# A fused layer with a routed mixture of experts: filler products once, the second expert's gathers behind the first's, and the fourth expert's table and gathers ahead of the first additions

## The reference, cut to what matters

```python
gate = jnp.sum(jax.nn.one_hot(top_idx, N_EXPERTS, dtype=jnp.float32) * top_w[..., None], axis=1)
y = jnp.zeros_like(t)
for e in range(N_EXPERTS):
    h = jax.nn.silu(t @ w1[e]) * (t @ w3[e])
    y = y + gate[:, e:e + 1] * (h @ w2[e])
x = layer_norm(ALPHA * x + y, ln2_g[l], ln2_b[l])
```

## Time and profile before

| | |
|---|---|
| median of 3 runs | 1004.55 us (1002.58 to 1005.56) |
| profiled execution | 1000.43 us |
| its span, first to last instruction | 998.8 us |
| mean granted TensorE clock | 0.975 of full speed |
| TensorE busy | 933.8 us, 93% of the span |
| VectorE, ScalarE, GpSimd busy | 606.9, 476.0, 200.1 us |

### The profile page before, as it was taken

How to read it: one execution, slowest core, us unless ns; L and a number is a source line. 1 busy time by engine, 2 the same in 40 slices (tenths; PEclk the granted TensorE clock), 3 DMA queues, 4 the chain that set the end, 5 groups by cost and what they waited for, 6 DMA issues and landing times.

```text
span 998.8 us, 19152 instructions
## 1 busy us (share of the span) xinstructions
PE 933.8 (93%) x7424; PEld 755.2 (76%) x7424; DVE 606.9 (61%) x793; ACT 476.0 (48%) x758; POOL 200.1 (20%) x244
## 2 busy tenths in 40 slices
PE   8999999999999999889998999899999999999930
PEld 7778998986777777668886678688888888888820
DVE  3203724655655664766656857577777777777728
ACT  3312622235655555551212446466666666666614
POOL 3000000000000000020000476634433333332116
PEclk9999999999999999989999999999999999999975
DMA  9301210002000301159332479999999999999656
GB/s 259 62 22 43 59 48 22 1 2 63 22 22 24 78 17 43 43 191 365 128 127 85 114 223 296 298 319 314 314 312 325 317 317 323 302 321 324 185 157 251
DMA packets 102666, 168.18 MB, mean 168 GB/s; under 512 B 25777, under 2 KB 49329, under 8 KB 102609
## 3 DMA queue, kind: packets, MB, share of 16 engines
q1 hardware_dynamic: 88768, 145.05, 43.0%
q0 software_dynamic: 10800, 21.17, 9.0%
q10 hardware_dynamic: 3040, 1.19, 0.6%
HBM read 142.84 MB, written 24.54 MB: 168 GB/s over the span
## 4 chain that ended last, share of the span: by engine, by line
PE 82%; DVE 5%; DMA 4%; POOL 4%; ACT 3%; issue 2%; SPq 0%; POOLq 0%; ACTq 0%; DVEq 0%
PE bank L705 14%; PE bank L707 13%; PE bank L706 13%; PE pz L705 6%; PE pz L707 6%; PE pz L706 6%; PE pz L1041 5%; PE pz L1083 3%; PE pz L821 3%; PE bank L901 3%; PE bank L917 2%; DMA tab<-slot_tokens 1%; POOL slot_tokens L581 1%; PE bank L1030 1%; DVE cstat L1784 1%
## 5 line engine op out<-in xcount | busy, mean ns | idle before, releaser
L1635 DVE TENSOR_TENSOR el<-er,eh 128x1024 fp32r<-128x1024 f32 x192 | 225.3, 1222 | 53.6 <-ACT eh L1334 53.1
L1334 ACT ACTIVATE eh<-er 128x1024 fp32r<-128x1024 f32 x192 | 190.4, 1052 | 0.0
L1568 DVE TENSOR_TENSOR_SCAN Qs<-Qs 128x128 f32<-128x128 f32 (+7 forms) x48 | 65.0, 1354 | 74.0 <-ACT Qs L1221 74.0
L705 PE MATMUL bank<-xT_hi,w_hi 128*128 128x512 f32 (+1 forms) x264 | 105.5, 400 | 1.9 <-DVE xT_lo L1453 1.9
L707 PE MATMUL bank<-xT_hi,w_lo 128*128 128x512 f32 (+1 forms) x264 | 101.7, 385 | 0.0
L705 PE MATMUL pz<-eh,xh 128*128 128x512 f32 x256 | 101.6, 397 | 0.0
L706 PE MATMUL bank<-xT_lo,w_hi 128*128 128x512 f32 (+1 forms) x264 | 101.3, 384 | 0.0
L706 PE MATMUL pz<-el,xh 128*128 128x512 f32 x256 | 99.8, 390 | 0.0
L707 PE MATMUL pz<-eh,xl 128*128 128x512 f32 x256 | 99.7, 389 | 0.0
L550 POOL MEMSET rw<- 128x128 f32 x1 | 0.2, 205 | 419.8 <-ACT aT L1262 419.8
L705 PE MATMUL bank<-w_hi,xT_hi 128*128 128x384 f32 x192 | 65.0, 338 | 1.3 <-ACT kteN L1236 1.3
(11 more groups left out here) (274 smaller groups left out, 1825.6 us busy)
## 6 DMA issues: line engine op xcount, KB each, us to landing
er<-in_w_dram SPq DMA_DIRECT2D x192, 512.0 KB, 9.6
w_raw<-in_w_in_dram SPq DMA_DIRECT2D x21, 512.0 KB, 4.0
x_row<-in_x_dram SPq DMA_DIRECT2D x8, 512.0 KB, 8.9
xres<-in_x_dram SPq DMA_DIRECT2D x8, 512.0 KB, 5.2
x_scratch<-x SPq DMA_DIRECT2D x8, 512.0 KB, 2.8
sum_scratch<-x SPq DMA_DIRECT2D x8, 512.0 KB, 3.9
cx<-sum_scratch SPq DMA_DIRECT2D x8, 512.0 KB, 6.5
out_dram<-cx SPq DMA_DIRECT2D x8, 512.0 KB, 2.6
```

The source lines that it names most:

```text
L705: pe.matmul(dst, lh, rh, start=(k == k_first), stop=False)
L1334: act.activation(eh[:, p, :], er[:, p, :], ACT.Copy).then_inc(S["eh_ok"], 1)
L1568: dve.tensor_tensor_scan(Qs[:, h, 0:W][:, ::-1], Qs[:, h, 0:W][:, ::-1], Qs[:, h, 0:W][:, ::-1], 1.0, ALU.mult, ALU.min).then_inc(S["scan_ ...
L1635: dve.tensor_tensor(el[:, p, :], er[:, p, :], eh[:, p, :].bitcast(F32), ALU.subtract).then_inc(S["el_ok"], 1)
```

## The change

1. `spin(34)` is taken out of `slot_tokens` and stands once, after the first two calls. The third call, in block 0, has none behind it.
2. `xgA` and `xgB` have a second pair of buffers, used by block 1. GpSimd issues block 1's gathers as soon as block 0's have landed, ahead of both scatters.
3. `slotG` has a second buffer, used by block 1.
4. Once the lists are written, GpSimd's order becomes: tables of 3, 0 and 1; quarters of 3, 0 and 1 (each waits for all three tables); gathers of 3; gates of 0 and 1; additions of 0; table and quarters of 2; additions of 1. Then `step` as before.
5. `gather` waits also for all earlier gathers to have landed.

```diff
-            for b in range(DIRECT):
...
+            def first_gather(b):
+
+                pool.wait_ge(S["first_ok"], 2 * b + 2)
+                for buf, src, ids in ((xgAs[b % 2], x1_dram, firstA), (xgBs[b % 2], x1_quarters, firstB)):
                     pool.indirect_dma_start(buf[:, :], None, src, bass.IndirectOffsetOnAxis(ids[:, b:b + 1], 0)).then_inc(S["xg_in"], 16)
+
+            first_gather(0)
+            pool.wait_ge(S["xg_in"], 32)
+            first_gather(1)
+            scatter(0)
+            scatter(1)
+            pool.wait_ge(S["xtr_ps"], NXR)
+            pool.wait_ge(S["xg_in"], 64)
+            first_gather(2)
...
             def pool_pass(j):
                 b0 = NE * j
-                load_table(0, b0)
-                load_table(1, b0 + 1)
-                quarters(0, b0, 2)
-                quarters(1, b0 + 1)
...
+                if isinstance(j, int):
+                    for r in (3, 0, 1):
+                        load_table(r, b0 + r)
+                    for r in (3, 0, 1):
+                        quarters(r, b0 + r, b0 + 3)
+                    gather(3, b0 + 3, 0, b0 + 1)
+                    gates(0, b0)
+                    gates(1, b0 + 1, 1)
+                    add_rows(0, b0)
+                    load_table(2, b0 + 2)
+                    quarters(2, b0 + 2, b0 + 4)
+                    add_rows(1, b0 + 1, 1)
...
                 last.then_inc(S["sids_ps"], 1)
-                if b:
-                    spin(34)
 
             for b in range(2):
                 slot_tokens(b)
+            spin(34)
```

More of the change, by code:

```diff
@@ L254, in build @@
         tabQ = [small(f"tabQ{r}", [P, 1], U32) for r in range(4)]
-        slotG = small("slotG", [P, 2])
+        slotGs = [small(f"slotG{r}", [P, 2]) for r in range(2)]
         quad = small("quad", [P, 1])
@@ L296, in build @@
         el = at("el", 48 * K, [P, NPIECE, D], F32R)
-        xgA = rt("xgA", 6 * K, [P, D])
-        xgB = rt("xgB", 10 * K, [P, DQ])
+        xgAs = [rt("xgA0", 6 * K, [P, D]), rt("xgA1", 42 * K, [P, D])]
+        xgBs = [rt("xgB0", 10 * K, [P, DQ]), rt("xgB1", 50 * K, [P, DQ])]
         xB = rt("xB", 11 * K, [P, NK, TR])
@@ L397, in experts_of @@
         def experts_of(eng, j, block):
-            block(NE * j, True)
+            block(NE * j, True, 0, 1)
             block(NE * j + 1, True, 1)
@@ L609, in load_table, with quarters, gather, gates @@
                     pool.dma_start(tab[r][g * TR:(g + 1) * TR, 2:4], idl_dram[bass.ds(b * TW + P, TR), :]).then_inc(S["idx_in"], 16)
-            def quarters(r, b, loaded=1):
-                pool.wait_ge(S["idx_in"], 16 * (1 + NQ) * (b + loaded))
+            def quarters(r, b, loaded=None):
+                pool.wait_ge(S["idx_in"], 16 * (1 + NQ) * (b + 1 if loaded is None else loaded))
                 pool.sem_inc(S["pool_go"], 1)
                 pool.tensor_scalar(tabQ[r][:, :], tab[r][:, 2:3], float(NQ), quad[:, 0:1], ALU.mult, ALU.add).then_inc(S["idxq_ok"], 1)
-            def gather(r, b):
-                pool.wait_ge(S["idxq_ok"], b + 1)
-                pool.wait_ge(S["xtr_ps"], NXR * b)
+            def gather(r, b, buf=0, ready=None):
+                pool.wait_ge(S["idxq_ok"], b + 1 if ready is None else ready)
+                pool.wait_ge(S["xtr_ps"], NXR * (b - buf))
+                pool.wait_ge(S["xg_in"], 32 * b)
                 pool.sem_inc(S["pool_go"], 1)
[L622 to L627, removed]
+                pool.indirect_dma_start(xgAs[buf][:, :], None, x1_dram, bass.IndirectOffsetOnAxis(tab[r][:, 0:1], 0)).then_inc(S["xg_in"], 16)
+                pool.indirect_dma_start(xgBs[buf][:, :], None, x1_quarters, bass.IndirectOffsetOnAxis(tabQ[r][:, 0:1], 0)).then_inc(S["xg_in"], 16)
+            def gates(r, b, buf=0):
+                pool.tensor_copy(slotGs[buf][:, :], tab[r][:, 1:4:2].bitcast(F32)).then_inc(S["slot_ok"], 1)
             def add_rows(r, b, buf=0):
@@ L637, in add_rows @@
                 if first_block(b):
-                    pool.tensor_scalar(yB[:, :], yB[:, :], slotG[:, 1:2], None, ALU.mult).then_inc(S["y_gated"], 1)
+                    pool.tensor_scalar(yB[:, :], yB[:, :], slotGs[buf][:, 1:2], None, ALU.mult).then_inc(S["y_gated"], 1)
                     pool.wait_ge(S["y_gated"], 1)
@@ L645, in add_rows @@
                 if first_block(b):
-                    pool.tensor_scalar(yA[:, :], yA[:, :], slotG[:, 0:1], None, ALU.mult).then_inc(S["y_gated"], 1)
+                    pool.tensor_scalar(yA[:, :], yA[:, :], slotGs[buf][:, 0:1], None, ALU.mult).then_inc(S["y_gated"], 1)
                     pool.wait_ge(S["y_gated"], 2)
@@ L659, in pool_pass @@
                 b0 = NE * j
-                load_table(0, b0)
-                load_table(1, b0 + 1)
-                quarters(0, b0, 2)
-                quarters(1, b0 + 1)
-                if not isinstance(j, int):
+                if isinstance(j, int):
[10 more added lines that the diff above has]
+                    add_rows(1, b0 + 1, 1)
+                else:
+                    for r in range(4):
+                        load_table(r, b0 + r)
+                    for r in range(4):
+                        quarters(r, b0 + r, b0 + 4)
                     gather(0, b0)
-                    gather(1, b0 + 1)
-                gates(0, b0)
-                if isinstance(j, int):
+                    gather(1, b0 + 1, 1)
+                    gather(2, b0 + 2)
+                    gates(0, b0)
                     add_rows(0, b0)
[L670 to L680, removed]
+                    gates(1, b0 + 1, 1)
+                    gather(3, b0 + 3)
+                    add_rows(1, b0 + 1, 1)
                 with pool.Fori(1, NE // 4) as i:
@@ L1016, in slot_tokens, with x_transposes @@
                 last.then_inc(S["sids_ps"], 1)
-                if b:
-                    spin(34)
             for b in range(2):
                 slot_tokens(b)
-            def x_transposes(b, rounds):
+            spin(34)
+            def x_transposes(b, rounds, buf=0):
+                xgA, xgB = xgAs[buf], xgBs[buf]
                 pe.wait_ge(S["xg_in"], 32 * b + 32)
@@ L1054, in rows_gu, with pe_block @@
                     last.then_inc(S["piece_done"], 1)
-            def pe_block(b, nxt, buf=0):
+            def pe_block(b, nxt, buf=0, nbuf=0):
                 pe.wait_ge(S["xTh_ok"], NXR * b + (1 if first_block(b) else NXR))
@@ L1067, in pe_block @@
                 if nxt:
-                    x_transposes(b + 1, (0, 1))
+                    x_transposes(b + 1, (0, 1), nbuf)
                 pe.wait_ge(S["hA_ok"], b + 1)
@@ L1073, in pe_block @@
                 if nxt:
-                    x_transposes(b + 1, (2,))
+                    x_transposes(b + 1, (2,), nbuf)
                 pe.wait_ge(S["hTB_ok"], b + 1)
@@ L1374, in x_hi, with act_block @@
                     act.activation(hi, src, ACT.Copy).then_inc(S["xTh_ok"], 1)
-            def act_block(b, nxt, buf=0):
+            def act_block(b, nxt, buf=0, nbuf=0):
                 piece_hi(b, 4)
@@ L1400, in act_block @@
                     act.wait_ge(S["slot_ok"], b + 1)
-                act.activation(yBs[buf][:, :], yB_bank, ACT.Copy, scale=1.0 if first_block(b) else slotG[:, 1:2])\
+                act.activation(yBs[buf][:, :], yB_bank, ACT.Copy, scale=1.0 if first_block(b) else slotGs[buf][:, 1:2])\
                     .then_inc(S["yB_ev"], 1)
@@ L1406, in act_block @@
                 act.wait_ge(S["rowsA_ps"], 2 * b + 2)
-                act.activation(yAs[buf][:, 512:], pp[1][:, :], ACT.Copy, scale=1.0 if first_block(b) else slotG[:, 0:1])\
+                act.activation(yAs[buf][:, 512:], pp[1][:, :], ACT.Copy, scale=1.0 if first_block(b) else slotGs[buf][:, 0:1])\
                     .then_inc(S["yA1_ev"], 1)
@@ L1735, in _, with dve_block @@
             row_gates(1)
-            def dve_block(b, nxt, buf=0):
+            def dve_block(b, nxt, buf=0, nbuf=0):
                 piece_lo(b, 4)
@@ L1765, in dve_block @@
                     dve.wait_ge(S["slot_ok"], b + 1)
-                    dve.tensor_scalar(yAs[buf][:, 0:512], pp[0][:, :], slotG[:, 0:1], None, ALU.mult).then_inc(S["yA0_ev"], 1)
+                    dve.tensor_scalar(yAs[buf][:, 0:512], pp[0][:, :], slotGs[buf][:, 0:1], None, ALU.mult).then_inc(S["yA0_ev"], 1)
             def dve_pass(j):
```

8 lines of the change are left out of this document (removed).

## The result

Nine executions of the changed kernel took 994.14 us in the median (993.11 to 1001.87), nine of the kernel before 1002.44 us (999.81 to 1005.56). The ratio is 0.9937, 95% interval 0.992 to 0.9954: 6.3 us (4.6 to 8.0), 0.6% faster. The profiled execution took 993.99 us with a span of 992.3 us, 6.5 us less than before.

What follows compares the result with a forecast made beforehand. TensorE, busy 93%, was taken to bound the kernel, with GpSimd the real bound ahead of block 3. 12.4 us saved less 5.0 us given back is 7.4 us: from median 1004.55 to 997.2 us, range 992.0 to 1001.5.

Steps and rivals of the forecast that it cites:

- What the change takes out: Three places in blocks 0 and 2 where TensorE stands still or runs filler; together 12.4 us saved.
- (a): Block 0: filler products take TensorE from 573.19 to 578.59 us; 5.4 us saved.
- (b): Block 0, transpose of `hB` to first A-row product: 1.5 us lost on block 1's gathers, saved.
- (c): Block 2, transpose of `hB` to first A-row product: 5.5 us lost on block 3's gathers, all saved.
- GpSimd's chain: GpSimd's new order from tables at 591.9 to block 1's A half of additions issued at 634.3, no further than before.
- The release: Block 2's evacuation on ScalarE, freed when block 1's additions land: 634.3 plus 7.5 us, so 641.8.
- First wait made: ScalarE's evacuation of block 1 waits from 607.0 for gates at 613.1; hidden from TensorE, 1.6 us to spare.
- Second wait made: Block 2's evacuation waits for block 1's additions; TensorE waits 3.2 us in block 3, plus 1.8 us clock: 5.0 us back.
- the pieces behind piece 1 cost nothing more: Block 3's later weight splits come every 1.2 us against 1.4 us of products, so TensorE loses nothing on them.
- Sum: Whole kernel: 12.4 us saved less 5.0 us given back, a gain of 7.4 us.
- The whole gain: Rival: quick landings hide block 2's late evacuation; gain 12.4 us, kernel at 992.2 us; chance 0.14.
- nearly all is given back: Rival: late links delay GpSimd's chain, with 5 us more the gain is 2.4 us, kernel at 1002.2 us; chance 0.14.

Runs made afterwards that it cites:

- Number 3: Kernel before with GpSimd's new order of tables and gathers alone, filler in its old place, block 1's gathers behind the first scatter; ratio 1.0001 (0.9981 to 1.002).
- numbers 1, 2 and 3: Kernel before with, in turn: filler taken out alone, 1.0011; whole change except GpSimd's new table order, 0.9996; that new order alone, 1.0001.
- numbers 5 to 10: Changed kernel with, in turn: filler back, 1.0099; gates first, 1.0004; chain shortened, 0.9942; shortened plus filler, 1.0017; shortened again, 0.9865; filler back again, 1.0019.

## Why the prediction was right, step by step

- **What the change takes out: right.** (a) and (b) were put at 6.9 us, and block 0 is 6.88 us shorter. (c) was put at 5.5; TensorE no longer waits for block 3's gathers.
- **GpSimd's chain: right at its end, by errors that cancel.** The release was put at 641.8 and came at 641.89. Part of that agreement is luck, since block 0 begins 1.0 us sooner in the trace after: counted from its start the release was put at 78.4 us and came at 79.5. TensorE was later as well, by the 1.4 us lost in blocks 1 and 2, and so the wait came out at 3.0 us against 3.2. In between the last scatter landed in 6.71 us instead of 4.2, so the tables began at 595.0 instead of 591.9; their landing took 5.06 us instead of 7.0, the three quarters 0.98 instead of 2.7; the A half was issued at 633.07 instead of 634.3 and landed in 8.80 us instead of 7.5, just outside my upper bound of 8.7.
- **First wait made: called hidden, and not quite.** ScalarE waited 5.51 us for the gates, until 611.53. I followed its effect only to piece 1 of `el`. It runs on through VectorE's queue to `hA`, where TensorE waited 0.83 us: block 2 has 1.0 us more than 23.93. Block 1 has 0.4 us, since TensorE waited for the gathers of block 2, which landed 11 us after their issue at 591.11; the prediction had given them no time of their own.
- **Second wait made: the size right (5.0 forecast, 5.5 measured), its make-up partly wrong.** I added a wait of 3.2 us at piece 1 and 1.8 us of clock. Both came, 3.0 us and the slow stretch. But the two don't add up to the loss. The sentence that the pieces behind piece 1 cost nothing more is the step that failed: `hA` stands on VectorE behind eleven pieces, the evacuation of the A rows and `hB`, 15.5 us from the release, and that set the end of the block, with the clock hidden behind it. Number 3 shows the other case. There the wait at the head was 1.5 us and the clock stayed up behind it; TensorE then waited 1.9 us for `hA`, the clock fell behind that wait and cost 1.6 us, and block 3 was as long (29.51 against 29.47 us). That the changed kernel's block would have been as long without the first fall is argued from this and was not run by itself.
- **Sum.** 7.4 us forecast; 5.4 us in the blocks and 6.3 us by the ratio, whose interval holds both. The difference in the blocks is 0.4 + 1.0 + 0.5 us, the three items above.
- **The rivals.** The whole gain did not come, as the landing of block 1's additions was longer than forecast (8.80 us against 7.5), not shorter. That nearly all is given back is what numbers 1, 2 and 3 show for the parts: each of the two halves of the change alone gained nothing that could be measured, and only together they did. I had treated them as terms of a sum.

## What to carry to other kernels

Before counting what a faster engine gains, write down the chain of the slow helper (here GpSimd: lists, table, gathers, additions, landing) and who waits for its last link; two edits on the two sides of such a chain are not terms of a sum, and have to be run together as well as apart (here nothing each, 5.4 us in the blocks together). Where an evacuation is released late, follow everything that is queued behind it on that engine and on the next, to the last instruction that the bounding engine needs, not to the first. And look at which earlier transfer a wait names: here one block's evacuation waited for a buffer that it didn't use, and mending that and the order of the gates and one table took another 4.7 us from the four blocks, on top of the change's 5.4.

## What the runs showed of the hardware that was not expected

- Indirect transfers landed later where other transfers were under way. The last scatter landed in 4.21 us before the change, with a DMA share of 0.39 from 586 to 592 us, and in 6.71 us after it, with 1.09 from 588 to 594 us. The additions of block 1 needed 8.8 us after the change, while 269 GB/s were moved (634 to 642 us), and up to 10.2 us in the experiments; the last additions of the kernel before needed 6.3 us at 73 GB/s (960 to 968 us).
- In all six traces taken on one chip (numbers 5 to 10) TensorE waited for its own instructions in block 0, mostly 0.3 to 1.2 us at a time, and the block was 38 to 52 us long instead of 24.7, or 30.1 with the filler. In the traces of all other numbers no such wait stands in that block. What makes the difference was not tried.
- A wait of 1.5 us for `el` in number 3 left the clock at 2.4 GHz, one of 1.9 us for `hA` 13 us later was followed by 4 us granted at 0.63 and 0.52 on the mean, partly at 1.2 GHz.
